# Preparing the first projection's input: three passes by token group, or one pass by feature tile

## The reference, cut to what matters

```
mod = silu(c) @ ada_w[l] + ada_b[l]
sh1, sc1, g1, sh2, sc2, g2 = [m[:, None, :] for m in jnp.split(mod, 6, axis=-1)]
csh1, csc1, ... = jnp.split(silu(c_ctx) @ ada_w[l] + ada_b[l], 6, axis=-1)
hc = modulate(rms_norm(ctx, norm1_g[l]), csh1, csc1)   # h * (1 + scale) + shift
hx = modulate(rms_norm(x, norm1_g[l]), sh1, sc1)
... split_proj(h @ lp["w_in"])                         # 26 tiles of 128 output features
```

## Time and the profile before

| | |
|---|---|
| median of 3 runs | 2264.8 us (2264.53 to 2266.89) |
| span of the profiled execution | 2265.7 us, from the first to the last instruction |
| its own time | not listed apart; the three runs lie from 1.2 us below to 1.2 us above that span |
| TensorE busy | 2050.2 us, 90% of the span |
| VectorE, ScalarE, GpSimd busy | 66%, 39%, 34% |
| mean granted TensorE clock | 0.957 of full speed |
| the prologue | TensorE starts the first matmul of the projection at 50.6 us and the tile `v` at 81.9 us |

### The profile page before, as it was taken

The page is one execution under the profiler, slowest core; times in us unless marked ns, Lnnn a source line. Parts: engine busy times, 40 slices in busy tenths (PEclk is TensorE's granted clock), DMA queues, the critical chain, the costliest instruction groups (busy, mean ns, idle before and its releaser), DMA issues. The chain is left out here.

```text
span 2265.7 us, 37012 instructions
## 1 busy us (share of the span) xinstructions
PE 2050.2 (90%) x15072; PEld 1594.0 (70%) x15072; DVE 1500.4 (66%) x2052; ACT 892.1 (39%) x1445; POOL 773.6 (34%) x460
## 2 busy tenths in 40 slices
PE   4989999837878898999999979999899999999898
PEld 1767677636767676788877768887677776776566
DVE  5777767679774548788988870454746676546644
ACT  5453443414434637333333331443434354333320
POOL 1144433300030145877777724533321111111111
PEclk7999999958899999999999999999999999999899
DMA  7535444597655422122221274523211111102512
GB/s 308 182 122 174 151 141 130 154 264 197 167 177 143 159 75 75 56 84 84 84 76 73 84 272 139 177 73 122 85 56 56 66 38 47 66 19 84 195 47 84
DMA packets 181335, 271.16 MB, mean 120 GB/s; under 512 B 74280, under 2 KB 122024, under 8 KB 176816
## 3 DMA queue, kind: packets, MB, share of 16 engines
q1 hardware_dynamic: 164816, 250.57, 33.9%
q10 hardware_dynamic: 16352, 18.22, 2.7%
HBM read 200.53 MB, written 68.23 MB: 119 GB/s over the span
## 5 line engine op out<-in xcount | busy, mean ns | idle before, releaser
L105 PE MATMUL b_ps<-h_hi,b_wpool 128*128 128x512 f32 (+1 forms) x896 | 277.4, 387 | 10.8 <-POOL b_wpool L744 10.8
L2995 PE MATMUL g_ps<-g_h_hi,w 128*128 128x512 f32 x784 | 260.0, 403 | 6.0 <-ACT g_q L3192 5.9
L3313 POOL TENSOR_TENSOR w<-raw_down,w 128x1024 fp32r<-128x1024 f32 x38 | 94.5, 2488 | 464.6 <-ACT w L3168 464.6
L2262 DVE SCALAR_TENSOR_TENSOR e_vars<-grid,vec,e_vars 128x1024 f32<-128x1024 f32 x168 | 216.0, 1285 | 7.4 <-ACT e_vars L2009 4.2
L105 PEld LDWEIGHTS b_ps<-h_hi,b_wpool 128*128 128x128 f32 x896 | 167.8, 192 | 56.3 <-POOL b_wpool L744 14.4
L2995 PEld LDWEIGHTS g_ps<-g_h_hi,w 128*128 128x128 f32 x784 | 149.3, 190 | 40.8 <-ACT g_q L3192 6.9
L105 PE MATMUL b_ps<-h_lo,b_wpool 128*128 128x512 f32 (+1 forms) x448 | 170.6, 381 | 0.0
L2995 PE MATMUL g_ps<-g_h_lo,w 128*128 128x512 f32 x392 | 156.1, 398 | 0.0
L2674 POOL TENSOR_TENSOR g_down_lo<-raw_down,g_down_hi 128x1408 fp32r<-128x1408 f32 x26 | 86.7, 3339 | 142.5 <-ACT g_down_hi L2574 142.5
L2513 PE MATMUL g_pb<-g_z_hi,g_down_hi 128*128 128x512 f32 x286 | 114.8, 401 | 14.7 <-DVE g_down_lo L2751 9.8
L744 POOL TENSOR_TENSOR b_wpool<-raw_in,b_wpool 128x1024 fp32r<-128x1024 f32 x26 | 67.9, 2611 | 173.2 <-ACT b_wpool L530 173.2
(11 more groups left out here) (524 smaller groups left out, 5284.4 us busy)
## 6 DMA issues: line engine op xcount, KB each, us to landing
e_raw_up<-w_ffn SPq DMA_DIRECT2D x22, 1024.0 KB, 4.9
raw_down<-w_down SPq DMA_DIRECT2D x32, 704.0 KB, 4.2
c_op<-ops SPq DMA_DIRECT2D x40, 512.0 KB, 5.0
raw_down<-w SPq DMA_DIRECT2D x38, 512.0 KB, 3.7
raw_in<-w SPq DMA_DIRECT2D x26, 512.0 KB, 4.2
mod_stage<-ada_rows ACTq DMA_DIRECT2D x24, 512.0 KB, 3.7
zs<-e_z SPq DMA_DIRECT2D x21, 512.0 KB, 2.6
ops<-b_xin SPq DMA_DIRECT2D x20, 512.0 KB, 4.7
```

What stands on the lines that cost most here:

```text
L105: last = nc.tensor.matmul(out, w[:, k, :], x[:, k, cols], start=(k == 0 and n == 0), stop=(k == nk - 1 and n == 2))
L2262: STT(out=acc, in0=view, scalar=wt, in1=acc, op0=ALU.mult, op1=ALU.add).then_inc(sem("conv"), 1)
L2995: mm = nc.tensor.matmul(out_bank, ww[w % 2][:, k], xx[g][:, k], start=(k == 0 and a == 0), stop=(k == KD - 1 and a == 2))
L3313: nc.gpsimd.tensor_tensor(w_lo[w % 2], raw[:, w % 2], w_hi[w % 2].bitcast(F32), ALU.subtract).then_inc(sem("lo"), 1)
```

## The change

The order of the prologue turns by a right angle: the vectors are finished feature tile by feature tile, and the inputs follow them.

- **`ada_w` by columns.** The host lays it out as 8 blocks, of which block `k` holds all 1024 rows of the 128 shift and the 128 scale columns of feature tile `k`. The loads are still 8 of 1 MB, but each goes to a place of its own list, and some wait for sums or for used blocks. `x` now comes first, in four pieces, then `ctx`, the first constants, and only then block 0. The second table of constants comes later.
- **`modulated(k)`** multiplies block `k`: 8 matmuls of 256 columns (4 of 512 before). ACT copies its rows (`rows_kept`), **`picked(k)`** turns them into columns by 8 small matmuls for each block (in all 4 before), and ACT makes shift and gain of tile `k` in two small instructions (`gains(k)`). DVE's `gains` is gone.
- **Inputs.** The pass `inputs_normed` is gone. DVE makes gain times root times input in one instruction for each piece (`input_pre`), ACT adds the shift and writes the high half (`input_high`), DVE makes the low half (`input_low`). A piece is a feature tile of one group; the 24 pieces come in the order of `PIECES`: groups 1 and 2 alternate, group 0 is last.
- **TensorE** interleaves: for a piece of group 1 it does `modulated(k + 2)`, the three matmuls of the piece for tile `w`, and `picked(k + 2)`; for other pieces only the three matmuls. The tile `g` is done whole after the last piece of groups 1 and 2, then `w` for group 0.
- ACT takes the logarithm and the root of the three groups one by one between other steps, and converts the tile `v` after the last piece and after silu of `c`, and the tile `k` after it has read tile `w` of group 0.

```diff
-    K_DVE = K_ORDER = tuple(range(KD))
+    PIECES = [(1, 0), (1, 1), (2, 0)] + [(g, k - (g - 1)) for k in range(2, KD) for g in (1, 2)] + [(2, KD - 1)]
+    PIECES += [(0, k) for k in range(KD)]
...
+            def load_ada(k):
+                if k in (2, 3):
+                    sp.wait_ge(sem("sumsq"), 1)
+                elif k in (4, 7):
+                    sp.wait_ge(sem("sumsq"), 2)
+                elif k in (5, 6):
+                    sp.wait_ge(sem("ada_used"), k - 4)
+                sp.dma_start(ada_place[k], d["ada"][k]).then_inc(sem(f"ada_in{k}"), 16)
...
+            for g in (1, 2):
+                for part in range(2):
+                    rows = slice(4 * part, 4 * part + 4)
+                    sp.dma_start(xin[:, rows, cols(g)], d["xT"][:, rows, seq(g)]).then_inc(sem(f"x{g}{part}"), 16)
             sp.dma_start(xin[:, :, 0:CTX], d["ctxT"]).then_inc(sem("x0"), 16)
             sp.dma_start(con, d["consts"][:, 0:NKEPT]).then_inc(sem("consts"), 16)
-            sp.dma_start(t["con_mixer"], d["consts"][:, NKEPT:NCON]).then_inc(sem("consts"), 16)
-            for g in (1, 2):
-                load_ada(g)
-                sp.dma_start(xin[:, :, cols(g)], d["xT"][:, :, seq(g)]).then_inc(sem(f"x{g}"), 16)
-            load_ada(3)
+            load_ada(0)
             load_w(("w", 0))
-            for i in range(4, GADA):
-                load_ada(i)
+            for kt in range(1, 4):
+                load_ada(kt)
+            load_w(("g", 0))
+            for kt in range(4, KD):
+                load_ada(kt)
...
+                for half in range(2):
                     for b in range(4):
+                        i = 4 * half + b
+                        mm = nc.tensor.matmul(rowps[k % 2][32 * b:32 * b + 2], silu_c[:, i, :], ada_cols[k][:, i], start=half == 0,
+                                              stop=half == 1)
+                mm.then_inc(sem("ada_used"), 1)
...
+                for x in range(2):
+                    for b in range(4):
+                        mm = nc.tensor.matmul(mod_cols[k % 2][:, x], mod_rows[k % 2][:, P * x:P * (x + 1)], t["c_ident"][:, 32 * b:32 * b + 2],
+                                              start=b == 0, stop=b == 3)
...
-            modulations()
-            first_dense("w", 0)
-            for g in (1, 2):
-                first_dense("wg", g)
+            sums(0, 1)
+            modulated(0)
+            sums(1, 2)
+            picked(0)
+            modulated(1)
+            sums(2, 0)
+            picked(1)
+            for g, kt in PIECES:
+                ahead = kt + 2 if g == 1 and kt + 2 < KD else None
+                if ahead:
+                    modulated(ahead)
+                if (g, kt) == (0, 0):
+                    for x in (1, 2):
+                        dense("g", 0, x)
+                first_dense(g, kt)
+                if ahead:
+                    picked(ahead)
...
-            squares(0)
-            squares(1)
+            for g in (1, 2):
+                for part in range(2):
+                    squares(g, part)
             act.wait_ge(sem("eps"), 2)
-            roots(0)
-            squares(2)
-            roots(1)
-            roots(2)
+            root_log(0, 1)
+            root(0, 1)
+            squares(0, 0)
+            rows_kept(0)
             hi("w", 0)
...
+            gains(0)
+            root_log(1, 2)
+            rows_kept(1)
+            root_log(2, 0)
+            root(1, 2)
+            gains(1)
+            root(2, 0)
+            for n, (g, kt) in enumerate(PIECES):
+                input_high(g, kt)
+                if g == 1 and kt + 2 < KD:
+                    rows_kept(kt + 2)
+                if n and PIECES[n - 1][0] == 1 and PIECES[n - 1][1] + 2 < KD:
+                    gains(PIECES[n - 1][1] + 2)
+                if (g, kt) == (1, 3):
+                    hi("g", 0)
...
             act.wait_ge(sem("c_in"), 16)
             A(c_row, c_row, ACT.Silu).then_inc(sem("c_row"), 1)
             hi("v", 0)
...
-            for g in range(3):
-                inputs(g)
+            folded(0, 1)
+            folded(1, 2)
+            folded(2, 0)
+            input_pre(*PIECES[0])
+            for n in range(NPIECES):
+                if n + 1 < NPIECES:
+                    input_pre(*PIECES[n + 1])
+                input_low(*PIECES[n])
```

More of the change, by code:

```diff
@@ L326, in _, with sums @@
         def _(pe):
-            def sums(g):
-                pe.wait_ge(sem("folded"), 2 * g + 2)
+            def sums(n, g):
+                pe.wait_ge(sem("folded"), 2 * n + 2)
+                if n == 0:
+                    pe.wait_ge(sem("consts"), 16)
+                elif g == 0:
+                    pe.wait_ge(sem("log"), 1)
                 for kt in range(2):
-                    mm = nc.tensor.matmul(ps[g][:, 0:width(g)], t["c_ones"], tmp[:, kt, cols(g)], start=kt == 0, stop=kt == 1)
+                    mm = nc.tensor.matmul(sums_ps[g][:, 0:width(g)], t["c_ones"], squared[g][:, kt], start=kt == 0, stop=kt == 1)
@@ L358, in first_dense @@
+            def first_dense(g, k):
+                pe.wait_ge(sem("h_lo"), piece[(g, k)])
+                i = chunk[("w", 0, g)]
+                if k == 0:
+                    pe.wait_ge(sem("lo"), tile_no[("w", 0)] + 1)
                     if i >= 4:
                         pe.wait_ge(sem("read_a"), act_read[CHUNKS[i - 4]])
[L360 to L369, removed]
+                w_hi, w_lo = weights(slot[("w", 0)])
+                out = ps[i % 4][:, 0:width(g)]
+                for n, (w, h) in enumerate(((w_hi, h_hi), (w_hi, h_lo), (w_lo, h_hi))):
+                    mm = nc.tensor.matmul(out, w[:, k, :], h[:, k, cols(g)], start=(k == 0 and n == 0), stop=(k == KD - 1 and n == 2))
+                if k == KD - 1:
+                    mm.then_inc(sem("chunk"), 1)
@@ new lines, in gains, with input_high @@
+            def gains(k):
+                act.wait_ge(sem("mod_cols"), k + 1)
+                if k == 0:
+                    act.wait_ge(sem("gain_of_bias"), 1)
+                A(t["mod"][:, :, k], mod_cols[k % 2][:, 0], ACT.Identity, bias=t["v_ada_b"][:, k:k + 1])
+                A(gain[:, :, k], mod_cols[k % 2][:, 1], ACT.Identity, scale=t["v_norm1_g"][:, k:k + 1],
+                  bias=gain_of_bias[:, k:k + 1]).then_inc(sem("gain"), 1)
+            def input_high(g, k):
+                act.wait_ge(sem("pre"), piece[(g, k)])
+                c = 1 if g == 0 else 0
+                A(h_hi[:, k, cols(g)], xin[:, k, cols(g)], ACT.Identity, bias=t["mod"][:, c, k:k + 1]).then_inc(sem("h_hi"), 1)
@@ new lines, in squares, with root_log, root @@
+            def squares(g, part):
+                rows = slice(4 * part, 4 * part + 4) if g else slice(0, KD)
+                act.wait_ge(sem(f"x{g}{part}" if g else "x0"), 16)
+                A(squared[g][:, rows], xin[:, rows, cols(g)], ACT.Square).then_inc(sem("squares"), 1)
+            def root_log(n, g):
+                act.wait_ge(sem("sumsq"), n + 1)
+                A(rstd[:, cols(g)], sums_ps[g][:, 0:width(g)], ACT.Ln, scale=1.0 / D, bias=t["c_eps"]).then_inc(sem("log"), 1)
+            def root(n, g):
+                act.wait_ge(sem("log"), n + 1)
+                A(rstd[:, cols(g)], rstd[:, cols(g)], ACT.Exp, scale=-0.5).then_inc(sem("rstd"), 1)
@@ L633, in _ @@
[L633 to L639, removed]
+            gains(0)
[13 more added lines that the diff above has]
+                    hi("g", 0)
+                if (g, kt) == (2, 6):
+                    for i in range(2):
+                        load_mod(i)
@@ L919, in gains @@
[L919 to L924, removed]
-                for c in range(2):
-                    a = STT(out=gain[:, c], in0=t["mod"][:, c, 8:16], scalar=1.0, in1=t["v_norm1_g"], op0=ALU.add, op1=ALU.mult)
-                a.then_inc(sem("gain"), 1)
-                dve.wait_ge(sem("gain"), 1)
-                dve.wait_ge(sem("normed"), 3)
@@ new lines, in input_pre, with input_low @@
+            def input_pre(g, k):
+                c = 1 if g == 0 else 0
+                dve.wait_ge(sem("gain"), k + 1)
+                if k == 0:
+                    dve.wait_ge(sem("rstd"), (3, 1, 2)[g])
+                STT(out=xin[:, k, cols(g)], in0=xin[:, k, cols(g)], scalar=gain[:, c, k:k + 1], in1=rstd[:, cols(g)], op0=ALU.mult,
+                    op1=ALU.mult).then_inc(sem("pre"), 1)
+            def input_low(g, k):
+                c = 1 if g == 0 else 0
+                dve.wait_ge(sem("h_hi"), piece[(g, k)])
+                STT(out=h_lo[:, k, cols(g)], in0=xin[:, k, cols(g)], scalar=t["mod"][:, c, k:k + 1], in1=h_hi[:, k, cols(g)].bitcast(F32),
+                    op0=ALU.add, op1=ALU.subtract).then_inc(sem("h_lo"), 1)
```

143 lines of the change are left out of this document (57 added, 86 removed).

## The result

The change made the kernel slower: 2283.8 us (median of 4 runs, 2279.2 to 2289.4) against 2264.7 for the kernel before, a ratio of 1.0082 with a 95% interval of 1.0059 to 1.0105. The forecast was 2267.4, so it missed by 16 us. Of its rivals, the one called half clock in the rounds had this time in its span of 2271 to 2290. The profiled execution has a span of 2285.4 us, 19.7 more than before.

The account below looks back on a forecast made before the run. The prediction took `ada_w` loads to bound the first 41 us, with TensorE nearly always busy after T. T 1.2 us later plus about 1.4 from the weight tiles gave +2.6 us: 2267.4 us median, range 2259 to 2278.

Parts of the forecast that it names:

- half clock in the rounds: Projection rounds: TensorE at half clock, 12 to 23 us more over six rounds if it never rises; chance 0.25.
- I take full level from about 24 on: Prologue: TensorE's granted clock was taken to be at full level from about 24 us on.
- a round: Prologue: `modulated`, a group 1 piece, `picked` and a group 2 piece; six of them at 4.6 to 4.7 us.
- T: Moment when TensorE has done tiles `w` and `g` and goes over to tile `v`: forecast 83.2 us, against 82.0 before.
- The first piece of the projection: Prologue: TensorE's first projection matmul forecast at 36.8 us, 13.8 us sooner than before.
- Two terms of the front: Before the first piece: ScalarE's logarithm table loaded during its wait, and `picked(0)` from 27.3 to 29.2 us.
- T to the end: After the prologue: what T gains or loses, the end gains or loses, with one correction for the weight tiles.
- The chain of weight tiles: Behind T: conversions and loads of `v`, `k`, `r` add about 1.4 us up to `turn_v` and cap any gain.
- POOL's slow low half: POOL's low half of `v` takes 6 us, delaying the load of `k` by 3 us: 2270.4 us; chance 0.1.
- Cheap picks: TensorE's picks cost 0.95 us each instead of 1.9, T is 76 and the median 2260.5 us; chance 0.2.
- the forecast sum: Prologue: 13.8 us won at the start against 14 us of picks, leaving T 1.2 us later.

Follow-up runs that it names:

- the wide pick: The change with its 8 matmuls per pick each streaming 128 columns instead of 2: ratio 1.0026 to the kernel before.
- Tile `g` in the rounds: The change with tile `g` multiplied piece by piece, three pieces behind tile `w`, instead of whole at the end: ratio 1.0102 to the kernel before.
- the change run again: The changed kernel without an edit, measured again on the chip of the follow-up runs: ratio 1.0084 to the kernel before.
- `g` in the rounds and early reads: The change with `g` piece by piece, silu of `c` before group 0, and `w` of groups 1 and 2 read between group 0's high halves: ratio 1.0097.
- Three versions: Two-matmul picks with `v` converted and read early (1.0031); also `g` piece by piece, 128-column picks, silu and `w` reads early (1.0032); also constants loaded early (1.0016).
- the kernel before with `v` read first: The kernel before, with ScalarE reading `v` of group 0 before it waits for weight tile `r`: ratio 0.9994 to the kernel before.
- One pick: The change with each pick done by 2 matmuls against the small summing matrix `sel` instead of 8 matmuls: ratio 1.0062 to the kernel before.
- the seven kernels with the tile `sel`: The changed kernel with two-matmul picks against a small summing matrix, alone or with further edits on top: ratios 1.0016 to 1.0062.
- `v` early: The change with two-matmul picks, and `hi("v", 0)` after the last high half of group 2, not behind silu of `c`: ratio 1.0031.

## Why the prediction was wrong

**The step that failed** is the one under the clock: "I take full level from about 24 on", against which half level in the rounds had been set as a rival with a chance of 0.25. Its price there, 12 to 23 us if the level never rose, is what happened, with two short rises. The argument against it was that a round has 2.5 us of other matmuls in 4.6, and that TensorE has hardly a gap. The trace shows both to be nearly true (one gap of 1.6 us in the rounds) and the level half all the same; the wide pick, the same instructions at the same places with 128 columns for 2, had it at 0.99 and 0.93. The Trainium skill ("TensorE: Matmul & The Clock Gate", Part 1), which says that the array's recent activity releases the clock, had pointed there, and the trace adds what the forecast lacked: TensorE busy by its records for 27.2 of 28 us did not release it (0.58). I had put this rival behind a row with a fall of the level after 1.06 us of picks and read that row as a gap, not as picks. Tile `g` in the rounds fits: half while the rounds were those of the change, full once its matmuls had joined (1.00 from 60 to 83 us, against 0.63). But narrow picks don't always hold the level down, since the change run again was at full from 71 us on, through its last two picks. What makes it rise in one round and not in another, these runs don't tell.

**The sum otherwise.** With the level full, T was 88.3 against a forecast of 83.2. The first piece of the projection came near 40 in the wide run, not at 36.8. Two terms of the front were mis-sized: ScalarE's table for the logarithm was not loaded during the wait, as I had read from before, but behind it (1.3 us; in the changed kernel it starts at 22.57, when the sum ends at 22.48), and the first pick ran at half level (3.66 for 1.9). They make 3.1 of the 5.1 us, and since the second is the level again, the clock's part in T is larger than the 12.1 us below. (The first sum of the wide run also began at 19.6, for 18.4, and ended 0.7 us late; the first matmul of the projection was 3.2 late in all, so these terms overlap.) Another 1.3 is the round with tile `g` (6.00 for 4.7), for which I have ScalarE's conversion and VectorE's pass of 2.33 us beside GpSimd's work as the cause, argued from the traces; 0.7 stays unassigned. The rest of the terms held: a pick 1.84 to 1.95 us (1.9), `modulated` 1.04 at full and 1.89 at half (1.1), a round 4.7, `g` 10.9 us (86.6 to 97.6 in the changed kernel), group 0 of `w` 2.9. In the changed kernel itself the first piece began at 39.3. What the change won at the start is so 11.3 us by the first matmul, not 13.8.

**T to the end.** The chain of weight tiles added 1.1 us between T and `turn_v` (1.4 forecast), and moving `hi("v", 0)` took back 1.2. The run with `g` in the rounds and early reads showed it as the cap that it was said to be. POOL's slow low half, a rival, didn't come: that of `v` took 2.63 us. Cheap picks, the other rival, didn't come either: 1.84 us at full level where it had 0.95.

**Where it went, in one line:** of T's 18.4 us, 12.1 are the level in the rounds (change against wide pick), 1.2 the forecast sum, which nets 14 us of picks against the sooner start, and 5.1 the mis-sized front and the one long round.

**Still open.** Three versions reached `turn_v` at 94.2, 91.6 and 89.2, two of them sooner than the kernel before (92.6), and their ratios are 1.0031, 1.0032 and 1.0016. The kernel before with `turn_v` 2.5 us sooner was not measurably faster either. In the profiles VectorE's first instruction of the recurrence (`c_lm`) starts at 487.1, 486.8 and 485.0, and at 488.9 in the kernel before, so the lead is still there when that stage begins. From there to the end the single profiles take 1783, 1781 and 1783 us, the kernel before 1777, and the kernel before with `v` read first 1786. This last one loses its lead inside the recurrence: it starts 6.3 us sooner, at 482.6, and its last `c_lm` starts at 736.9 against 737.0. So a stage that the edits don't touch moves by up to 9 us from one profiled execution to the next, for the kernel before too, and one profile of each can't tell whether some of it belongs to the new order. The chain of waits there wasn't taken apart.

A second thing stands open, and it bears on all versions built on one pick. One pick and the wide pick reach T at 87.8 and 88.3 and `turn_v` at 100.1 and 100.5, yet their ratios are 1.0062 and 1.0026. Take from each ratio what its `turn_v` explains: in the seven kernels with the tile `sel`, 1.5 to 8.2 us are left (5.6 in the mean); in the six runs without it (the change counted twice), -2.0 to 4.3 (0.6 in the mean). `turn_v` is that of one profile each. So some 5 us seem to come with `sel` or the two-matmul pick, outside the prologue. No run tested this; wide picks of 8 matmuls with `v` early, `v` read first and early reads would.

## What to carry to other kernels

Read busy time and granted clock together: many small matmuls with full loads of weights and few columns keep TensorE busy by its records and can leave its clock at half, and then they nearly double the price of the dense work woven between them: 12 us here, on top of the 14 us that the picks take at full level. If such work must be interleaved, let each instruction stream more columns than needed (T 12.1 us sooner here), or make it few instructions (12.6). And when a pass is turned to "as it arrives", count what each arrival now repeats (here a turn of rows into columns, 128 records where 8 were) and follow the in-order programs of the other engines behind it: with tile `g` in the rounds 9 us won on TensorE were given back, once to a read and once to a weight tile that stood later in ScalarE's program.

## What the runs showed of the hardware

- A pick of 16 records with loads of 128 columns took 1.84 us streaming 2 columns and 1.95 streaming 128, both at full level; at half 3.41 with 2 columns and, in the one place that shows it, 3.66 with 128. The extra 126 columns were nearly free.
- With TensorE busy 27.2 of 28 us the granted clock was 0.58; with 23.8 of 28, and picks of 128 columns for 2, it was 0.99.
- A fused pass of VectorE over 128 by 512 values took 0.75 us and, while GpSimd made a low half beside it, up to 2.84.
